# An encoder in four runs: transposing the next run's inputs inside the output projection

## The chip, the core and the metric

The kernel runs on one core of one Trainium2 chip. Times are device microseconds (us) of one execution; lower is better. TensorE (PE) multiplies matrices and writes PSUM, VectorE (DVE) and ScalarE (ACT) read PSUM and work on SBUF, GpSimd (POOL) works on SBUF, and SyncE (SP) issues most transfers. Each engine takes its instructions in program order, and semaphores tie the engines together.

## The reference, cut to what matters

Two batches go through the same two-layer encoder, a prompt of 512 tokens and a sample of 1024 tokens, 1024 features wide.

```
def encoder_layer(x, ...):
    h = x @ w_in                            # 1024 x 2912, cut into twelve parts
    oa = window_attn(...) * silu(a_g)
    ob = mla(...) * silu(b_g)
    oc = neighborhood_attn(...) * silu(c_g)
    o = concatenate([oa, ob, oc]) @ w_out   # 1024 x 1024
    return layer_norm(ALPHA * x + o, ln_g, ln_b)
```

So the kernel has four runs: layer 0 on the prompt (run 0, 512 tokens) and on the sample (run 1, 1024 tokens), then layer 1 on the prompt (run 2) and on the sample (run 3). Run s+1 never reads what run s writes: the input of run s+1 is the output of run s-1 (the input norm for run 1), which lies in HBM in `y_out`.

## The kernel before

**Tiles.** Tokens go in tiles of 128: a run has NT = 4 or 8 of them. Each large product is made of three float32r matmuls: both factors are split into a high part and a low part (`x_hi`, `x_lo`, `w_hi`, `w_lo`), and high x high, high x low and low x high are added up in PSUM. `products` (L562 to L567) issues them all. `x_hi` and `x_lo` hold 1024 token columns and are used twice in a run: first for the run's transposed input, and at its end for the gated attention output.

**Input of a run.** SP loads tile t of the input from HBM into `x_place[t]` (`load_x`, L1362; seven tiles right after the last attention scores of the run before, L1481 to L1483; an eighth shares the place of tile 0 and is loaded at the start of its run, L1409 to L1411). PE transposes a tile with eight 128x128 transposes into two PSUM banks out of banks 4 to 7 (`transposes`, L569 to L576, key "xT"). ACT copies each half into `x_hi` (`high_part`, L791), DVE subtracts that from PSUM into `x_lo` and frees the bank (`low_part`, L1010). In the kernel before all this stands at the start of a run: tiles 0 to 3, then, ahead of the first two pieces of the first weight unit, tiles 4, 5 and 6, 7 (`rest_of_x`, L709 to L713). Ahead of piece 0 PE also waits until tiles 2 and 3 are read (`wait_parts`).

**Weights.** They come in units of 256 columns, twelve for the input projection ("ck" is the first, "aq0" the second) and four for the output projection ("o0" to "o3"). For each unit SP loads two halves, ACT makes `w_hi` (`split_high`, L828) and `w_lo` is made by POOL for half 0 and by DVE for half 1 (`split_low`, L452, the subtraction stands in L456). One exception: at the start of runs 1 to 3 POOL makes both halves of ck (L1282 to L1284). PE waits for both halves before it begins a unit. ck has two pieces of 24 matmuls (128x512) for 512 tokens and four for 1024.

**Output projection and norm.** `out_order` (L160) gives the order of PE's tiles: (0, t) for all t, (1, t) for all t, and then (2, t) and (3, t-1) in turns; each is 24 matmuls (128x256) into one of banks 0 to 3. DVE adds each into `z` (L1217). After (3, t) DVE takes the statistics of token tile t (`norm_stats`), then `norm_coef` of tile t-1 and `norm_gain` of tile t-2, a product with ln_g (L980); ACT makes the square root (`norm_sqrt`, L775) and the scaling (`norm_rows`, L771); POOL adds ln_b (`bias_rows`, `norm_bias`, L1249), and SP stores the tile. The last three tiles' gain and bias stand in the next run (`norm_tail`, L1078; `norm_last_rows`, L820; L1285).

**POOL's order at a boundary**, which this change leaves alone, is:

```
                for i in range(len(IN_UNITS) + 1, NU):
                    split_low(pool, s, i, 0)              # o1, o2, o3, half 0
                pool.wait_ge(lnp_loaded, 32 * (s + 1))
                bias_rows(s, range(NT - 1 if s == RUNS - 1 else NT - 3))
                # next run, i = 0:
                    split_low(pool, s, i, 0)              # ck, half 0
                    if s and i == 0:
                        split_low(pool, s, 0, 1)          # ck, half 1
                        bias_rows(s - 1, range(NTILES[s - 1] - 3, NTILES[s - 1]))
```

So POOL adds the bias of tile 0 (runs of four tiles) or of tiles 0 to 4 (runs of eight) ahead of ck's `w_lo`, the bias of the last three tiles behind it, and then makes aq0's half 0.

Of the kernel before, what the change touches and what calls it, by code (L numbers as in the profile page):

```python
# [29 lines left out]
RUNS = len(SEQ_LEN)  # L30
# [134 lines left out]


def pe_steps(ph, s):


    n = len(units_of(ph, s)) // 2  # L170
    steps = []
    late = 1 if dense_wide(ph, s) else 2
    for j in range(n + late):
        if j < n:
            steps.append(("S", 2 * j))
            if ph != "B":
                steps.append(("S", 2 * j + 1))
        if 0 <= j - 1 < n:
            steps.append(("T", j - 1, 0))
        if j - late >= 2 and (j - late) % 2 == 0:  # L180
            steps.append(("R", (j - late) // 2 - 1))
        if j < n and ph == "B":
            steps.append(("S", 2 * j + 1))
        if 0 <= j - 1 < n and late == 1:
            steps.append(("T", j - 1, 1))
        if 0 <= j - late < n:
            steps.append(("V", j - late))
    return steps + [("R", n // 2 - 1)]
# [17 lines left out]
def encoder_kernel(nc, ins, y_out):  # L206
# [18 lines left out]
    with ctx:  # L225
# [84 lines left out]
        for s, NT in enumerate(NTILES):  # L310
            for t in range(NT):
                for hf in range(2):
                    uses.take(("xT", s, t, hf), 4 + (2 * t + hf) % 4)
            for u in IN_UNITS:
                if u in TOKEN_UNITS:
                    for t in range(NT):
                        take_mm((u, s, t))
                else:
                    for c, j in feature_order(s, u):
                        take_mm((u, s, j, c))  # L320
# [28 lines left out]
            for u, t in out_order(s):  # L349
                take_mm(("out", s, u, t))  # L350

        def halves(s, ph):
# [59 lines left out]
        group_no = Numbered(all_groups)  # L412
        xh_no = Numbered([("xT", s, t, i) for s in range(RUNS) for t in range(NTILES[s]) for i in range(2)])
        split_no = Numbered([(s, u) for s in range(RUNS) for u in UNITS])
# [145 lines left out]
        def _(pe):  # L560
# [138 lines left out]
            for s, NT in enumerate(NTILES):  # L699

                def x_tiles(tiles):
                    for t in tiles:
                        if s:
                            pe.wait_ge(xin_loaded[t], loads_of(t, 1, s))
                        else:
                            pe.wait_ge(pre_ln[4], t + 1)
                        transposes(s, "xT", t)

                def rest_of_x(n):  # L709
                    if n % 2 == 0:  # L710
                        wait_parts(s, "xT", 2 * n)
                    if NT > 4 and n < 2:
                        x_tiles((4 + 2 * n, 5 + 2 * n))  # L713
                if s == 0:
                    pe.wait_ge(ident_loaded, 16)
                x_tiles(range(4))
                if s == 0:
                    pe.wait_ge(pre_const, 16 * 5)
                    nc.tensor.matmul(bank[0][0:A_HEADS, :], t5_sb, onehot, start=True, stop=True).then_inc(pre_mm, 1)
                    pe.wait_ge(pre_neg, 1)  # L720
# [29 lines left out]
                for n, t in out_order(s):  # L750
# [7 lines left out]
                    for h in range(2):  # L758
                        if n == 0 and h == 1:
# [3 lines left out]
                                                             (x_hi[:, k, q_tile(t)], w_lo[:, i % 2, k, :]),  # L763
                                                             (x_lo[:, k, q_tile(t)], w_hi[:, i % 2, k, :]))])


        @block.scalar
        def _(act):
# [4 lines left out]
            def norm_sqrt(sems, k):  # L773
                act.wait_ge(sems[0], k + 1)
                nc.scalar.activation(ln_sd[:, k % 12:k % 12 + 1], ln_mv[:, k % 12, 1:2], ACT.Sqrt, bias=eps[:, 0:1]).then_inc(sems[1], 1)  # L775

            def norm_steps(sems, bufs, k):

                for n, buf in enumerate(bufs):
                    norm_sqrt(sems, k + n)  # L780
                    if n:
                        norm_rows(sems, bufs[n - 1], k + n - 1)

# [58 lines left out]
            for s, NT in enumerate(NTILES):  # L842
                split_high(s, 0)
                for t in range(NT):
                    high_part(s, t)
                if s:
                    norm_last_rows(s - 1)
                split_high(s, 1)
# [100 lines left out]
                split_high(s, NU - 2)  # L949
                split_high(s, NU - 1)  # L950
                norm_steps(layer_ln, [z_place(t) for t in range(NT - 1)], ln_no[s, 0] - 1)
                if s == RUNS - 1:
# [4 lines left out]
        def _(dve):  # L957
# [127 lines left out]
            for s, NT in enumerate(NTILES):  # L1085
                if s == 0:
                    split_low(dve, s, 0, 1)
                for t in range(NT):
                    low_part(s, t)
                if s:  # L1090
                    norm_tail(s - 1)
                split_low(dve, s, 1, 1)
                if s == 0:
# [113 lines left out]
                for n, t in out_order(s):  # L1207
# [11 lines left out]
                    if n == 3:  # L1219
# [6 lines left out]
                        if 1 < t < NT - 1:  # L1226
                            norm_gain(ln_norm, ln_gain, z_place(t - 2), k - 2, qkC[:, 0, :])
                if s == RUNS - 1:
                    norm_tail(s)
# [98 lines left out]
        def _(sp):  # L1328
# [55 lines left out]
            for s, NT in enumerate(NTILES):  # L1384
# [96 lines left out]
                if s + 1 < RUNS:  # L1481
                    for t in range(min(NTILES[s + 1], 7)):
                        load_x(s + 1, t)  # L1483
# [89 lines left out]
```

## Time and profile before

| | us |
|---|---|
| median of 3 runs | 1938.62 |
| lowest, highest | 1937.54, 1939.48 |
| the profiled execution, its time | 1935.7 |
| its span, first to last instruction | 1933.9 |

The time of the profiled execution is its span and 1.8 us around it. Times within the trace count from the span's start. "Boundary 0-1" is the stretch from the last output matmul of run 0 to the steady matmuls of run 1's input projection; boundaries 1-2 and 2-3 likewise.

### The profile page before, as it was taken

To read this page: it belongs to the slowest core of one execution; us is meant where nothing else is said; L and a number is where in the kernel's file an instruction comes from. 1 tells how busy PE (TensorE), PEld (TensorE's weight loads), DVE (VectorE), ACT (ScalarE), POOL (GpSimd) and SP (SyncE) were. 2 spreads that over 40 slices of the span, in tenths; PEclk is the share of its full clock that TensorE was granted. 3 is DMA by queue.
4 is the path that set the end of the run, shared out by engine and by line. 5 is a ranking of instruction groups with operands and counts; after the bars stand their busy time and mean duration, and the time that the engine had idled before them with its cause. 6 is when DMAs were issued, how large, how long until landed. Compare 5 with 4: busy or idle time off the path is not lost.

```text
span 1933.9 us, 31986 instructions
## 1 busy us (share of the span) xinstructions
PE 1830.6 (95%) x12530; PEld 1482.0 (77%) x12530; DVE 957.2 (49%) x2247; ACT 787.9 (41%) x1675; POOL 433.6 (22%) x491
## 2 busy tenths in 40 slices
PE   3999988999999998999989999999999999989996
PEld 2896578889986664889979865888898766578896
DVE  4365654311425875555452475460133287555636
ACT  3344653321124666443142366342112266644512
POOL 3352402310110062001152213140111103500103
PEclk9999999999999999999999999999999999989998
DMA  6666134221126020006145350621212151000222
GB/s 205 208 214 193 26 120 120 76 66 44 45 66 156 9 62 0 1 2 197 45 147 192 103 149 1 202 82 55 66 45 66 49 138 38 25 1 2 84 70 87
DMA packets 148163, 167.15 MB, mean 86 GB/s; under 512 B 18304, under 2 KB 134400, under 8 KB 147504
## 3 DMA queue, kind: packets, MB, share of 16 engines
q1 hardware_dynamic: 146080, 158.75, 27.4%
q0 software_dynamic: 1152, 4.19, 0.5%
q8 instruction: 102, 1.67, 0.4%
q10 hardware_dynamic: 784, 2.16, 0.3%
q14 instruction: 45, 0.37, 0.1%
HBM read 143.00 MB, written 32.65 MB: 91 GB/s over the span
## 4 chain that ended last, share of the span: by engine, by line
PE 87%; DVE 7%; ACT 3%; issue 1%; POOL 1%; DMA 1%; SPq 0%; DVEq 0%; ACTq 0%
PE psum L565 64%; PE psum L685 8%; PE psum L655 8%; PE psum L637 5%; DVE nmax L1025 2%; PE psum L696 1%; DVE pt_sb L1050 1%; ACT pAC L809 1%; DVE x_lo L1016 1%; DVE qB_lo L1182 1%; POOL gT L1249 0%; DMA qA<-x_prompt 0%; PE psum L575 0%; ACT qB_hi L931 0%; PE psum L551 0%
## 5 line engine op out<-in xcount | busy, mean ns | idle before, releaser
L565 PE MATMUL psum<-w_hi,x_hi 128*128 128x256 f32 x1344 | 379.9, 283 | 8.8 <-DVE x_lo L1205 6.7
L565 PE MATMUL psum<-w_hi,x_lo 128*128 128x256 f32 x1344 | 381.0, 284 | 0.0
L565 PE MATMUL psum<-w_lo,x_hi 128*128 128x256 f32 x1344 | 380.6, 283 | 0.0
L565 PE MATMUL psum<-x_hi,w_hi 128*128 128x512 f32 x816 | 325.8, 399 | 10.4 <-DVE hT L1095 7.8
L565 PE MATMUL psum<-x_lo,w_hi 128*128 128x512 f32 x816 | 325.2, 399 | 0.0
L565 PE MATMUL psum<-x_hi,w_lo 128*128 128x512 f32 x816 | 325.2, 398 | 0.0
L456 POOL TENSOR_TENSOR w_lo<-w_stage,w_hi 128x1024 fp32r<-128x1024 f32 (+1 forms) x83 | 164.3, 1990 | 651.1 <-ACT w_hi L839 651.0
L456 DVE TENSOR_TENSOR w_lo<-w_stage,w_hi 128x1024 fp32r<-128x1024 f32 (+1 forms) x77 | 141.4, 1852 | 323.4 <-ACT w_hi L839 323.4
L565 PEld LDWEIGHTS psum<-w_hi,x_hi 128*128 128x128 f32 x1344 | 255.7, 190 | 10.4 <-issue 10.2
L565 PEld LDWEIGHTS psum<-w_lo,x_hi 128*128 128x128 f32 x1344 | 254.4, 189 | 0.2
L565 PEld LDWEIGHTS psum<-w_hi,x_lo 128*128 128x128 f32 x1344 | 253.7, 189 | 0.0
L839 ACT ACTIVATE w_hi<-w_stage 128x1024 fp32r<-128x1024 f32 (+1 forms) x160 | 129.4, 859 | 228.7 <-PE psum L565 160.4
L565 PEld LDWEIGHTS psum<-x_hi,w_hi 128*128 128x128 f32 x816 | 154.8, 190 | 50.2 <-DVE hT L1095 9.5
L816 ACT ACTIVATE pt_sb<-psum 128x256 f32<-128x256 f32 (+2 forms) x224 | 113.4, 506 | 189.2 <-PE psum L655 186.5
L565 PEld LDWEIGHTS psum<-x_hi,w_lo 128*128 128x128 f32 x816 | 154.7, 190 | 37.8
L565 PEld LDWEIGHTS psum<-x_lo,w_hi 128*128 128x128 f32 x816 | 154.8, 190 | 37.3
L1273 POOL COPY rinv_wide<-rinv 128x256 f32<-128x256 f32 x96 | 38.5, 401 | 629.5 <-DVE rinv L1056 629.5
L809 ACT ACTIVATE pAC<-pAC,nmax 128x385 f32<-128x385 f32 (+3 forms) x288 | 164.3, 573 | 22.7 <-DVE nmax L1042 13.3
L1025 DVE TENSOR_REDUCE nmax<-psum 128x1 f32<-128x1024 f32 (+1 forms) x96 | 100.5, 1047 | 122.0 <-PE psum L565 120.6
L655 PEld LDWEIGHTS psum<-ident,pAC 128*128 128x128 f32 x768 | 81.8, 142 | 83.2 <-ACT pAC L809 73.2
L1050 DVE COPY pt_sb<-psum 128x256 f32<-128x256 f32 (+2 forms) x224 | 127.3, 568 | 11.0 <-PE psum L655 11.0
L655 PE MATMUL psum<-ident,pAC 128*128 128x128 f32 x768 | 123.3, 288 | 7.9 <-ACT pAC L809 6.8
(141 smaller groups left out, 2651.7 us busy)
## 6 DMA issues: line engine op xcount, KB each, us to landing
w_stage<-w_in SPq DMA_DIRECT2D x48, 512.0 KB, 4.6
w_stage<-w_in SPq DMA_DIRECT2D x88, 256.0 KB, 3.4
toep<-rpb_tile SPq DMA_DIRECT2D x12, 1152.0 KB, 15.0
rpb_tile<-rpb_col SPq DMA_DIRECT2D x48, 192.0 KB
hT<-y SPq DMA_DIRECT2D x18, 512.0 KB, 12.0
y<-hT SPq DMA_DIRECT2D x18, 512.0 KB, 2.7
w_stage<-w_out SPq DMA_DIRECT2D x32, 256.0 KB, 4.1
w_stage<-w_out SPq DMA_DIRECT2D x16, 512.0 KB, 5.0
```

What stands on the lines that cost most here:

```text
L456: last = eng.tensor_tensor(lo, src, hi.bitcast(F32), ALU.subtract)
L565: last = nc.tensor.matmul(out, w, x, start=(n == 0 and part != 1), stop=(n == len(pairs) - 1 and part != 0))
L637: nc.tensor.matmul(ps[:, 0:n], w, x, start=True, stop=True).then_inc(full(("S", s, u, 0)), 1)
L655: last = nc.tensor.transpose(ps[:, (c % 4) * P:(c % 4 + 1) * P], src[:, c * P:(c + 1) * P], ident[:, :])
L685: last = nc.tensor.matmul(bank[b][64 * k:64 * k + 64, cols], value_tile(s, u, c), pt_sb[:, slot, (c % 4) * P:(c % 4 + 1) * P], start=(c == ...
L696: last = nc.tensor.transpose(bank[b][:, 256 + P * m:256 + P * m + P], rinv_wide[:, P * m:P * m + P], ident[:, :])
L809: nc.scalar.activation(pAC[:, i % 3, 0:m], pAC[:, i % 3, 0:m], ACT.Exp, bias=nmax[:, j:j + 1], scale=-1.0, accum_out=psums[:, j:j + 1]).th ...
L816: nc.scalar.activation(pt_sb[:, half_index[s, (u, hf)] % 4, 0:n], ps[:, 0:n], ACT.Copy).then_inc(pt_act, 1)
L839: last = nc.scalar.activation(hi, src, ACT.Copy)
L1025: nc.vector.tensor_reduce(nmax[:, j:j + 1], b_scores(s, i), AX.XY, ALU.min).then_inc(score_done, 1)
L1050: nc.vector.tensor_copy(pt_sb[:, half_index[s, (u, hf)] % 4, 0:n], ps[:, 0:n]).then_inc(pt_dve, 1)
L1273: nc.gpsimd.tensor_copy(rinv_wide[:, :].rearrange("p (u n) -> p u n", u=4), rinv[:, at:at + 4].unsqueeze(2).broadcast_to([P, 4, 64])).then ...
```

## The change

The next run's tiles are transposed and split while the output projection of the run ahead is under way. `next_x` says which tile follows which output tile: tile t after (3, t) for t up to 3, and, where the next run has eight tiles, tile 4 after (1, 1), tile 5 after (1, 3) and tile 6 after (2, 1). Tile 7 stays at the start of its run, ahead of piece 1 of ck. PE, ACT and DVE each take their part at that place in their own order. ACT's steps of the norm are no longer a block behind `split_high` of o3 but stand in the loop over `out_order`; `split_high` of the next run's ck follows (2, NT-1); `norm_last_rows` and `norm_tail` come first in the next run. SP loads the tiles of a run of 1024 tokens in the order 4, 5, 6, 0, 1, 2, 3. POOL's list of instructions stays as it is.

```
+def x_order(s):
+
+    return (4, 5, 6, 0, 1, 2, 3, 7) if s and NTILES[s] > 4 else tuple(range(NTILES[s]))
+
+
+def next_x(s, n, t):
+
+    if s + 1 == RUNS:
+        return ()
+    if n == 3 and t < min(NTILES[s], NTILES[s + 1]):
+        return (t,)
+    if NTILES[s + 1] > NTILES[s]:
+        return {(1, 1): (4,), (1, 3): (5,), (2, 1): (6,)}.get((n, t), ())
+    return ()
+
+
+def x_at_start(s):
+
+    return (7,) if s and NTILES[s] > 4 else () if s else range(NTILES[s])
...
                     if n % 2 == 0:
                         wait_parts(s, "xT", 2 * n)
-                    if NT > 4 and n < 2:
-                        x_tiles((4 + 2 * n, 5 + 2 * n))
+                    if s and n == 1:
+                        x_tiles(s, x_at_start(s))
                 if s == 0:
                     pe.wait_ge(ident_loaded, 16)
-                x_tiles(range(4))
-                if s == 0:
+                    x_tiles(s, x_at_start(s))
...
                              [p for k in range(4 * h, 4 * h + 4) for p in ((x_hi[:, k, q_tile(t)], w_hi[:, i % 2, k, :]),
...
+                    x_tiles(s + 1, next_x(s, n, t))
...
-                split_high(s, 0)
-                for t in range(NT):
+                if s == 0:
+                    split_high(s, 0)
+                else:
+                    norm_last_rows(s - 1)
+                for t in x_at_start(s):
                     high_part(s, t)
-                if s:
-                    norm_last_rows(s - 1)
                 split_high(s, 1)
...
-                split_high(s, NU - 1)
-                norm_steps(layer_ln, [z_place(t) for t in range(NT - 1)], ln_no[s, 0] - 1)
+                for n, t in out_order(s):
+                    if (n, t) == (1, NT - 1):
+                        split_high(s, NU - 1)
+                    if n == 3 and t < NT - 1:
+                        k = ln_no[s, t] - 1
+                        norm_sqrt(layer_ln, k)
+                        if t:
+                            norm_rows(layer_ln, z_place(t - 1), k - 1)
+                    for x in next_x(s, n, t):
+                        high_part(s + 1, x)
+                    if (n, t) == (2, NT - 1) and s + 1 < RUNS:
+                        split_high(s + 1, 0)
...
-                for t in range(NT):
-                    low_part(s, t)
                 if s:
                     norm_tail(s - 1)
+                for t in x_at_start(s):
+                    low_part(s, t)
                 split_low(dve, s, 1, 1)
...
                             norm_gain(ln_norm, ln_gain, z_place(t - 2), k - 2, qkC[:, 0, :])
+                    for x in next_x(s, n, t):
+                        low_part(s + 1, x)
...
                 if s + 1 < RUNS:
-                    for t in range(min(NTILES[s + 1], 7)):
+                    for t in x_order(s + 1)[:7]:
                         load_x(s + 1, t)
```

The bookkeeping of banks (`take_x`) and of the count of `x_hi` halves (`xh_no`) follows the new order.

## Rows read from the trace of the kernel before

**Rows 1.** Page: the span, and part 1, busy time, share of span and count.

```profile
span 1933.9 us, 31986 instructions
...
PE 1830.6 (95%) x12530; PEld 1482.0 (77%) x12530; DVE 957.2 (49%) x2247; ACT 787.9 (41%) x1675; POOL 433.6 (22%) x491
```

**Rows 2.** Chain that ended last, by time: start, length, engine, tile, line.

```profile
346.98 254.68 PE psum L565 x1368
...
997.15 119.16 PE psum L565 x648
```

**Rows 3.** Timeline, PE, boundary 0-1: start, length, engine, line, names, count [idle before <-releaser].

```profile
329.09 1.91 PE L575 MATMUL psum<-ident,qA 128*128 128x128 f32 x16
333.27 2.36 PE L575 MATMUL psum<-ident,qA 128*128 128x128 f32 x16 [2.27 <-DVE x_lo L1016]
...
339.36 0.48 PE L565 MATMUL psum<-x_hi,w_hi 128*128 128x512 f32 x1
...
345.07 1.04 PE L575 MATMUL psum<-ident,kA 128*128 128x128 f32 x8
345.94 1.04 PE L575 MATMUL psum<-ident,qA 128*128 128x128 f32 x8
346.73 0.48 PE L565 MATMUL psum<-x_hi,w_hi 128*128 128x512 f32 x1
```

**Rows 4.** Timeline, POOL, boundary 0-1.

```profile
330.02 2.36 POOL L1249 TENSOR_TENSOR hT<-hT,qkC 128x1024 f32<-128x1024 f32 x1 [19.47 <-DVE hT L980]
332.35 4.69 POOL L456 TENSOR_TENSOR w_lo<-w_stage,w_hi 128x1024 fp32r<-128x1024 f32 x2
```

**Rows 5.** Windows: length, busy us (count) of each engine, PEclk, DMA share, GB/s.

```profile
294.40:329.10 34.70, 34.70 (x289) 34.61 (x290) 14.46 (x29) 7.93 (x10) 4.79 (x2) 1.00 0.28 81
984.50:987.90 3.40, 3.40 (x10) 2.66 (x9) 3.40 (x3) 1.41 (x4) 3.16 (x1) 0.51 0.49 144
```

**Rows 6.** Timeline, DVE, boundary 0-1: tile (3, 2), its gain, and tile (3, 3).

```profile
326.42 0.42 DVE L1217 SCALAR_TENSOR_TENSOR hT<-hT,psum 128x256 f32<-128x256 f32 x1 [2.46 <-PE psum L565]
...
328.67 1.22 DVE L980 TENSOR_TENSOR hT<-hT,qkC 128x1024 f32<-128x1024 f32 x1
329.80 0.42 DVE L1217 SCALAR_TENSOR_TENSOR hT<-hT,psum 128x256 f32<-128x256 f32 x1
```

**Rows 7.** Timeline, ACT, boundary 0-1: the high parts of tiles 0 to 3.

```profile
331.83 4.44 ACT L794 ACTIVATE x_hi<-psum 128x512 fp32r<-128x512 f32 x8
```

**Rows 8.** Timeline, POOL, boundary 2-3.

```profile
1274.75 4.67 POOL L456 TENSOR_TENSOR w_lo<-w_stage,w_hi 128x1024 fp32r<-128x1024 f32 x2
```

**Rows 9.** Timeline, PE, boundary 2-3: the first matmul of ck's piece 1.

```profile
1289.13 0.48 PE L565 MATMUL psum<-x_hi,w_hi 128*128 128x512 f32 x1
```

**Rows 10.** Timeline, POOL, boundary 1-2.

```profile
975.86 2.37 POOL L1249 TENSOR_TENSOR hT<-hT,qkC 128x1024 f32<-128x1024 f32 x1 [3.38 <-DVE hT L980]
978.18 4.70 POOL L456 TENSOR_TENSOR w_lo<-w_stage,w_hi 128x1024 fp32r<-128x1024 f32 x2
984.74 9.43 POOL L1249 TENSOR_TENSOR gT<-gT,qkC 128x1024 f32<-128x1024 f32 x3 [1.86 <-DVE gT L980]
994.12 2.98 POOL L456 TENSOR_TENSOR w_lo<-w_stage,w_hi 128x512 fp32r<-128x512 f32 x2
```

**Rows 11.** Timeline, DVE, boundary 1-2: one gain alone, and the last three.

```profile
974.57 1.22 DVE L980 TENSOR_TENSOR hT<-hT,qkC 128x1024 f32<-128x1024 f32 x1
...
983.44 5.66 DVE L980 TENSOR_TENSOR gT<-gT,qkC 128x1024 f32<-128x1024 f32 x3
```

**Rows 12.** Timeline, PE, boundary 1-2: matmuls of ck at either clock.

```profile
983.46 0.47 PE L565 MATMUL psum<-x_hi,w_hi 128*128 128x512 f32 x1 [1.93 <-DVE x_lo L1016]
...
985.23 0.63 PE L565 MATMUL psum<-x_hi,w_hi 128*128 128x512 f32 x1
985.66 0.63 PE L565 MATMUL psum<-x_lo,w_hi 128*128 128x512 f32 x1
```

**Rows 13.** Transfers: issue, count, KB each, median us from issue to landing.

```profile
qA<-y SPq DMA_DIRECT2D x14, 512.0 KB, 4.4
```

More of the change, by code:

```diff
@@ L310, in encoder_kernel, with take_x @@
         for s, NT in enumerate(NTILES):
-            for t in range(NT):
+            def take_x(s, t):
                 for hf in range(2):
                     uses.take(("xT", s, t, hf), 4 + (2 * t + hf) % 4)
+            if s == 0:
+                for t in range(NT):
+                    take_x(s, t)
             for u in IN_UNITS:
@@ L318, in encoder_kernel @@
                 else:
-                    for c, j in feature_order(s, u):
+                    for n, (c, j) in enumerate(feature_order(s, u)):
+                        if u == "ck" and n == 1:
+                            for t in x_at_start(s) if s else ():
+                                take_x(s, t)
                         take_mm((u, s, j, c))
@@ L350, in encoder_kernel @@
                 take_mm(("out", s, u, t))
+                for x in next_x(s, u, t):
+                    take_x(s + 1, x)
         def halves(s, ph):
@@ L412, in encoder_kernel @@
         group_no = Numbered(all_groups)
-        xh_no = Numbered([("xT", s, t, i) for s in range(RUNS) for t in range(NTILES[s]) for i in range(2)])
+        xh_no = Numbered([("xT", s, t, i) for s in range(RUNS) for t in x_order(s) for i in range(2)])
         split_no = Numbered([(s, u) for s in range(RUNS) for u in UNITS])
@@ L699, in _, with x_tiles @@
             for s, NT in enumerate(NTILES):
-                def x_tiles(tiles):
+                def x_tiles(s, tiles):
                     for t in tiles:
@@ L775, in norm_sqrt @@
                 nc.scalar.activation(ln_sd[:, k % 12:k % 12 + 1], ln_mv[:, k % 12, 1:2], ACT.Sqrt, bias=eps[:, 0:1]).then_inc(sems[1], 1)
[L777 to L782, printed above, removed]
             act.wait_ge(pre_mem, 2)
@@ L842, in _ @@
             for s, NT in enumerate(NTILES):
-                split_high(s, 0)
-                for t in range(NT):
+                if s == 0:
+                    split_high(s, 0)
+                else:
+                    norm_last_rows(s - 1)
+                for t in x_at_start(s):
                     high_part(s, t)
-                if s:
-                    norm_last_rows(s - 1)
                 split_high(s, 1)
@@ L1087, in _ @@
                     split_low(dve, s, 0, 1)
-                for t in range(NT):
-                    low_part(s, t)
                 if s:
                     norm_tail(s - 1)
+                for t in x_at_start(s):
+                    low_part(s, t)
                 split_low(dve, s, 1, 1)
```

## The prediction

> **What bounds the kernel now.** The page comes first: of a span of 1933.9 us PE is busy for 95% [rows 1], so what PE does not do itself matters only where PE waits. The change touches three such places, the boundaries between runs. In the chain of waits the long PE stretches behind boundaries 0-1 and 1-2 run without a break, 254.68 us from 346.98 and 119.16 us from 997.15 [rows 2]; what arrives late at a boundary is not made up there. So I measure each boundary by one moment: the first matmul of ck's piece 1 at 0-1 (346.73, [rows 3]) and at 2-3 (1289.13, [rows 9]), and the first matmul of aq0 at 1-2 (997.15, [rows 2]). The timelines of PE, POOL and DVE are then read for what sets that moment.
>
> At 0-1 the output matmuls end at 329.09. Transposes follow in blocks with a wait of 2.27 us for `x_lo` in between, ck starts at 339.36, and a second block of 16 transposes, 345.07 to 346.73, parts pieces 0 and 1 [rows 3]. Beside it POOL adds the bias of tile 0 from 330.02 to 332.38, as soon as DVE's gain has run, and makes both halves of ck's `w_lo` by 337.04 [rows 4]. The weights are thus ready 2.3 us ahead of the inputs. That is all the room there is.
>
> **The change, part by part.** *Transposes.* Eight take 345.94 - 345.07 = 0.87 us [rows 3]. None is removed: 64 stay for a run of eight tiles, 32 for one of four. They move into a stretch in which PE is already busy for 34.70 of 34.70 us with a matmul every 0.12 us [rows 5], so each tile put in stretches it by 0.87 us. Bounds: 0, if they slipped into gaps, and 0.87; I take 0.87, since the row shows no gap. What they save is the wait for `x_lo`.
>
> *What stands behind the stretch.* Ahead of (3, 2) at 0-1 lie the transposes of tiles 4, 5, 6, 0 and 1: 5 x 0.87 = 4.35 us. DVE's gain of tile 0 belongs to the step of (3, 2), 2.25 us behind its first instruction [rows 6], and POOL's bias of tile 0 waits for that gain [rows 4]. POOL's order is unchanged and ck's `w_lo` is queued behind that bias. So the weights come 4.35 us later: 337.04 + 4.35 = 341.4. This takes the place of the wait that was removed. ACT's `w_hi` of ck, now behind (2, 3), is earlier than before and of no help, because POOL is held by the bias.
>
> *Boundary 0-1.* PE starts ck at 341.5 (0.1 us for the hand-over), piece 0 takes 345.07 - 339.36 = 5.71 us [rows 3], tile 7's eight transposes 0.87: piece 1 starts at 348.1 against 346.73, **+1.3 us** with rounding. Tile 7's load is issued behind the store of tile 0, at some 337, and lands 4.4 us later [rows 13], well ahead of 347. The next latest is `x_lo` of tile 3: (3, 2) reaches DVE at 326.42 + 4.35 = 330.8; its step takes 329.80 - 326.42 = 3.38 us [rows 6]; `low_part` of tile 2 waits about 0.7 us for ACT (a scaling, then a high part of 4.44/8 = 0.56 us, [rows 7]) and takes as an estimate 1.2; then the step of (3, 3) without a gain, 3.38 - 1.22 = 2.2, and again 1.2: 339.5. So even with weights in time PE would start ck no earlier than it does now.
>
> *Do DVE and ACT keep up?* A step of PE is two output tiles and a transposed one: 48 x 0.12 + 0.87 = 6.6 us. DVE's is 3.38 + 0.42 + 0.7 + 1.2 = 5.7 [rows 6]. They do; with four banks for the output tiles I cost these edits, the new order of `norm_sqrt` and `norm_rows` and the new order of loads at 0. If that cover were gone, PE would stop for a bank.
>
> *Boundary 2-3.* The same shape: `w_lo` ended at 1279.42 [rows 8] and ends at 1283.8; piece 1 starts at 1283.9 + 5.71 + 0.87 = 1290.5 against 1289.13 [rows 9]: **+1.3 us**.
>
> *Boundary 1-2.* Run 2 has four tiles, put behind (3, 0) to (3, 3), so (3, 6), whose step holds the gain of tile 4, comes 4 x 0.87 = 3.5 us later. POOL's bias of tile 4 ended at 978.2 [rows 10] and ends at 981.7. Then `w_lo` of ck, 4.70 us [rows 10]: 986.4 at best. Before, ck started at 983.46 [rows 12]. DVE's last three gains now come right then, no longer behind the `low_part`s. One gain alone takes 1.22 us, three beside POOL's bias took 5.66 [rows 11], while POOL's three biases took 9.43 where three alone take 3 x 2.37 = 7.1 [rows 10]: the two engines hold each other up. Bounds for ck's weights: 986.4 with no gain in between, 986.4 + 2 x 1.22 = 988.8 with two; I take one, 987.6. The Trainium skill (SBUF — State Buffer, section "SBUF: two separate sides") calls the port that DVE and GpSimd share an exclusive lock, which the engine that starts first holds for its whole instruction; the trace agrees, with 5.66 and 9.43 us. Without such a lock this boundary would come out 1.2 us lower.
>
> Two pieces of ck take 2 x 24 x 0.238 (5.71/24) = 11.4 us. Behind an idle PE the clock comes in: between 984.50 and 987.90 the granted clock was 0.51 of full, the 1.2 GHz level, after PE had waited for `x_lo` until 983.46 [rows 5, 12], and a matmul took 985.66 - 985.23 = 0.43 us instead of 0.238. That stretch cost 3.4 x (0.43 - 0.238)/0.43 = 1.5 us. The new wait, from 978.5 to 987.6, is longer than that one, so the 1.5 us stay: ck ends at 987.6 + 11.4 + 1.5 = 1000.5. POOL needs until about the same time: from 978.2 to 997.1 it was idle for 1.86 us [rows 10], so the same work from 981.7 on ends at 998.8, or 1000 with the gain moved in. aq0 starts at 1000.4 against 997.15: **+3.2 us** (bounds +1.6 and +5).
>
> *The clock at 0-1 and 2-3.* Before, waits of 2.27 us between blocks of transposes left it at full [rows 3]. Now PE has nothing from the transposes of tile 3 (about 335.2) to 341.5, over 6 us. Bounds: 0, if the slow stretch falls into the wait itself, and 3.0, two stretches; I take 1.2, near to the 1.5 of the one seen: **+2.4 us** for both. The Trainium skill (TensorE: Matmul & The Clock Gate, "What's actually happening") says that the throttled state is the default and that activity releases it; the stretch at 0.51 behind a wait agrees.
>
> **The sum.** 1.3 + 1.3 + 3.2 + 2.4 = +8.2 us. The profiled execution, 1935.7 us, would take 1943.9. It lies 2.9 us under the median of 1938.62; against the median the forecast is 1946.8 us. A measurement of this kernel can tell a change of 0.2%, 3.9 us, from none.
>
> **The rivals.** *A, the clock stays up and POOL and DVE do not meet.* Then only the waits for POOL are left: 1.3 + 1.3 + 1.6 = +4.2, 1942.8 us. For it: at 0-1 waits of 2.27 us did nothing to the clock. Against it: the new waits are nearly three times as long.
> *B, the transposes slip into PE's queue* and stretch nothing. Then the weights come as before: ck starts at 337.2 and piece 1 at 343.8, -3.0; at 2-3 1279.5 + 6.6 = 1286.1, -3.0; at 1-2 POOL, rid of its 1.86 us of idle time, has aq0's half at about 996, -1.1: -7.1, **1931.5 us, faster**. It decides from the point where a tile stretches the output projection by less than some 0.4 us: 2.3 us of room over five tiles. For it: busy PE need not be PE at its peak. Against it: a matmul every 0.12 us without a gap [rows 5].
> *C, DVE falls behind.* If ACT's scaling delays a high part by over 1 us more, the 0.9 us of room in a step is gone; each of the twelve steps of (3, t) with a transposed tile, four at each boundary, could cost 0.4 us: +5 on top, 1951.8 us. Against it: the sum of 5.7 in 6.6 us.
>
> **Chances.** The forecast 0.66, A 0.16, B 0.08, C 0.10. A lies just past the bound of 0.2%, so most of it counts as no change: faster 0.07, same 0.14, slower 0.79. The range starts below A, less what runs differ by (1 us to either side), and takes in the two upper bounds, +5 at 1-2 and part of C: 1940.0 to 1952.5 us.
>
> **What would show it.** In the changed profile: PE's output stretch longer by 5.2 us (six tiles) at 0-1; POOL's bias of tile 0 at about 334.4 and ck's `w_lo` ending at about 341.4; ck's first matmul released by POOL's `w_lo` and no longer by `x_lo`, at all three boundaries, after an idle stretch of PE of over 6 us; a granted clock of about half behind it. I am wrong if PE's first ck matmul follows the last transposes at once, if the output stretch does not grow, or if the wait is for `x_lo`.

## The result, and the profile after

| | before | changed kernel |
|---|---|---|
| median, us | 1937.54 | 1942.93 |
| lowest, highest | 1933.22, 1941.13 (7 runs) | 1939.94, 1945.58 (7 runs) |
| profiled execution: time, span | 1935.7, 1933.9 | 1941.06, 1939.3 |

The ratio of the two is **1.003 [1.0015, 1.0044]**: slower by 5.4 us, between 2.9 and 8.5. The forecast was +8.2 us, slower.

From the page of the changed kernel, the span and the line of busy times:

```profile
span 1939.3 us, 31986 instructions
...
PE 1828.4 (94%) x12530; PEld 1483.5 (76%) x12530; DVE 957.5 (49%) x2247; ACT 787.7 (41%) x1675; POOL 434.8 (22%) x491
```

As many instructions as before, PE busy for 2 us less, a span longer by 5.4 us [rows 1]: nothing was added, PE waits more. The diff moves line numbers: the products are L595 here (L565 before), the transposes L605 (L575), the low halves of weights L486 (L456), POOL's bias L1285 (L1249), DVE's gain L1014 (L980), `low_part` L1050 (L1016).

The chain of waits at boundary 0-1, then at 1-2 (start, us, what):

```profile
332.78 1.14 DVE hT L1014
...
334.05 2.36 POOL hT L1285
336.42 4.63 POOL w_lo L486 x2
...
341.13 8.25 PE psum L595 x24
...
350.26 254.68 PE psum L595 x1368
...
987.28 3.37 issue
990.65 132.34 PE psum L595 x696
```

In the chain of before [rows 2] the long stretch began at 346.98; here it begins at 350.26 and is just as long. What leads to it reads as a sentence: DVE's gain of tile 0, POOL's bias of tile 0, POOL's two low halves of ck, PE. At 0-1 the transposes of the other tiles no longer stand in the chain.

PE's timeline at the three boundaries (start, length, what; in brackets the idle time ahead of it and what ended it):

```profile
341.13 0.77 PE L595 MATMUL psum<-x_hi,w_hi 128*128 128x512 f32 x1 [6.10 <-POOL w_lo L486]
341.70 0.63 PE L595 MATMUL psum<-x_lo,w_hi 128*128 128x512 f32 x1
...
346.39 0.43 PE L595 MATMUL psum<-x_hi,w_hi 128*128 128x512 f32 x1
...
350.01 0.48 PE L595 MATMUL psum<-x_hi,w_hi 128*128 128x512 f32 x1
...
990.65 0.76 PE L595 MATMUL psum<-x_hi,w_hi 128*128 128x512 f32 x1 [8.74 <-issue]
...
1291.11 0.76 PE L595 MATMUL psum<-x_hi,w_hi 128*128 128x512 f32 x1 [6.09 <-POOL w_lo L486]
```

ck waits for 6 to 9 us at each boundary. Before there were two waits of about 2 us each, for `x_lo`, with a block of transposes in between [rows 3, 12]. Behind the wait the matmuls run 0.63 us long, and start 0.43 apart, until 346.39, then 0.39 to 0.40 long.

The windows over those slow stretches, and over the output stretch of run 0 (busy time and count of PE, PEld, DVE, ACT, POOL, then granted clock, DMA share, GB/s):

```profile
339.50:346.30 6.80, 5.17 (x12) 4.13 (x13) 6.80 (x4) 1.24 (x1) 5.64 (x3) 0.51 0.67 199
984.60:994.80 10.20, 4.14 (x10) 3.31 (x11) 10.08 (x6) 3.73 (x5) 10.20 (x5) 0.51 0.51 159
1288.40:1295.20 6.80, 4.09 (x10) 3.25 (x11) 6.76 (x7) 2.20 (x2) 5.63 (x3) 0.51 0.83 241
294.18:333.88 39.70, 39.70 (x336) 39.70 (x336) 20.76 (x39) 15.54 (x22) 4.81 (x2) 1.00 0.27 73
```

The granted clock is at the 1.2 GHz level behind all three waits; in the first profile of before only behind the one at 1-2 [rows 5]. The output stretch, 34.70 us in before [rows 5], is 39.70 long and still full.

POOL's timeline at 0-1 and 1-2:

```profile
334.05 2.36 POOL L1285 TENSOR_TENSOR hT<-hT,qkC 128x1024 f32<-128x1024 f32 x1 [23.63 <-DVE hT L1014]
336.37 4.66 POOL L486 TENSOR_TENSOR w_lo<-w_stage,w_hi 128x1024 fp32r<-128x1024 f32 x2
...
982.62 2.34 POOL L1285 TENSOR_TENSOR hT<-hT,qkC 128x1024 f32<-128x1024 f32 x1 [3.35 <-DVE hT L1014]
984.92 5.64 POOL L486 TENSOR_TENSOR w_lo<-w_stage,w_hi 128x1024 fp32r<-128x1024 f32 x2
990.52 9.51 POOL L1285 TENSOR_TENSOR gT<-gT,qkC 128x1024 f32<-128x1024 f32 x3
```

and DVE's, the last low parts at 0-1 and the last three gains at 1-2:

```profile
338.02 1.28 DVE L1050 TENSOR_TENSOR x_lo<-psum,x_hi 128x512 fp32r<-128x512 f32 x2
...
985.19 9.76 DVE L1014 TENSOR_TENSOR gT<-gT,qkC 128x1024 f32<-128x1024 f32 x3
```

At 1-2 DVE's gains and POOL's low halves run beside each other: the two low halves take 5.64 us in place of 4.66, and the three gains, which also meet POOL's biases, 9.76 in place of 3 x 1.22.

**All profiles in one table.** I cut each trace at the same matmuls of PE, counted from the start of the kernel, and took the time from cut to cut. "0-1" runs from the first matmul of output tile (1, 0) to the first of ck's third piece, "1-2" from the first of (3, 0) to the first of the unit behind aq0, "2-3" like 0-1. "3a" is run 3 from there to the matmul at 1669.66 in before, "3b" from that to the one at 1840.00. Worked out from PE's timelines; us:

```
                       0-1     1-2     2-3      3a      3b
before               58.11   73.82   58.36   374.82  170.34
before, again        60.24   74.31   60.42   374.82  170.33
changed              61.54   77.20   61.07   373.35  166.80
changed, again       61.08   76.59   61.08   373.35  166.85
e1                   60.49   76.74   60.66   373.34  171.01
e2                   59.22   76.49   59.22   373.35  170.00
e3                   60.29   78.12   61.35   373.34  168.71
e3, again            62.07   77.99   59.21   373.36  170.82
e4                   57.47   73.41   57.47   373.34  168.77
f1                   52.84   75.56   52.83   373.34  170.97
f2                   52.83   73.54   52.75   373.34  170.11
```

Between the two first profiles the boundaries cost 3.43 + 3.38 + 2.71 = +9.5 us, and run 3 gives 1.47 + 3.54 = 5.0 of it back; the +0.9 that is missing to the 5.4 of the spans lies elsewhere, most of it in run 2. Between the two second profiles the boundaries cost only 0.84 + 2.28 + 0.66 = +3.8, run 3 gives 5.0 back, and the changed kernel is the shorter one by 0.5 us. One pair of profiles is thus no measure of the whole; the ratio above, of seven executions each, is. Run 3 has no run behind it, and the change does nothing in these two stretches: the granted clock decides it (below).

### The profile page after: what moved, and what is told of

Same layout as the page of the kernel before. It is cut to its first block, busy times and chain, and to the rows that moved or that the text cites. A ratio compares the mean times of both kernels' runs of the same rounds, so it can differ in the third digit from the quotient of the medians.

```text
span 1939.3 us, 31986 instructions
## 1 busy us (share of the span) xinstructions
PE 1828.4 (94%) x12530; PEld 1483.5 (76%) x12530; DVE 957.5 (49%) x2247; ACT 787.7 (41%) x1675; POOL 434.8 (22%) x491
## 4 chain that ended last, share of the span: by engine, by line
PE 88%; DVE 6%; ACT 3%; issue 1%; POOL 1%; DMA 1%; SPq 0%; DVEq 0%; ACTq 0%; POOLq 0%
PE psum L595 64%; PE psum L715 8%; PE psum L685 8%; PE psum L667 5%; DVE nmax L1059 2%; PE psum L726 1%; DVE pt_sb L1084 1%; ACT pAC L832 1%; PE psum L605 1%; POOL w_lo L486 1%; DVE qB_lo L1216 0%; DMA qA<-x_prompt 0%; PE psum L581 0%; ACT qB_hi L955 0%; POOL hT L1285 0%
## 5 line engine op out<-in xcount | busy, mean ns | idle before, releaser
L595 PE MATMUL psum<-w_hi,x_hi 128*128 128x256 f32 x1344 | 381.4, 284 | 8.2 <-DVE x_lo L1239 6.7
L595 PE MATMUL psum<-w_hi,x_lo 128*128 128x256 f32 x1344 | 381.0, 283 | 0.0
L595 PE MATMUL psum<-w_lo,x_hi 128*128 128x256 f32 x1344 | 380.2, 283 | 0.0
L595 PE MATMUL psum<-x_hi,w_hi 128*128 128x512 f32 x816 | 328.0, 402 | 29.1 <-POOL w_lo L486 12.2
L595 PE MATMUL psum<-x_lo,w_hi 128*128 128x512 f32 x816 | 326.8, 401 | 0.0
L595 PE MATMUL psum<-x_hi,w_lo 128*128 128x512 f32 x816 | 326.7, 400 | 0.0
L486 POOL TENSOR_TENSOR w_lo<-w_stage,w_hi 128x1024 fp32r<-128x1024 f32 (+1 forms) x83 | 166.2, 2012 | 673.7 <-ACT w_hi L862 673.6
L486 DVE TENSOR_TENSOR w_lo<-w_stage,w_hi 128x1024 fp32r<-128x1024 f32 (+1 forms) x77 | 134.4, 1762 | 335.0 <-ACT w_hi L862 334.9
L595 PEld LDWEIGHTS psum<-w_hi,x_hi 128*128 128x128 f32 x1344 | 255.5, 190 | 9.6 <-issue 9.4
L595 PEld LDWEIGHTS psum<-w_lo,x_hi 128*128 128x128 f32 x1344 | 254.7, 189 | 0.2
L595 PEld LDWEIGHTS psum<-w_hi,x_lo 128*128 128x128 f32 x1344 | 253.6, 189 | 0.0
L595 PEld LDWEIGHTS psum<-x_hi,w_hi 128*128 128x128 f32 x816 | 156.1, 191 | 69.2 <-issue 21.5
L595 PEld LDWEIGHTS psum<-x_hi,w_lo 128*128 128x128 f32 x816 | 155.8, 191 | 38.3
L595 PEld LDWEIGHTS psum<-x_lo,w_hi 128*128 128x128 f32 x816 | 156.2, 191 | 37.7
```

Of the source, the lines that this page charges most:

```text
L486: last = eng.tensor_tensor(lo, src, hi.bitcast(F32), ALU.subtract)
L595: last = nc.tensor.matmul(out, w, x, start=(n == 0 and part != 1), stop=(n == len(pairs) - 1 and part != 0))
```

## Experiments

Two theories. **Mine:** the loss is PE's wait for POOL, which is held by the bias of the first tile, and the clock that falls behind the wait. **Rivals:** the transposes cost more inside the output projection than outside it, or the new order of ACT, DVE or SP costs by itself.

### e1: POOL makes ck's low halves ahead of the bias

```
                 for i in range(len(IN_UNITS)):
-                    split_low(pool, s, i, 0)
+                    if s == 0 or i:
+                        split_low(pool, s, i, 0)
...
-                        split_low(pool, s, 0, 1)
...
-                bias_rows(s, range(NT - 1 if s == RUNS - 1 else NT - 3))
+                if s == RUNS - 1:
+                    bias_rows(s, range(NT - 1))
+                else:
+                    ahead = 3 if NT > 4 else 0
+                    bias_rows(s, range(ahead))
+                    split_low(pool, s + 1, 0, 0)
+                    split_low(pool, s + 1, 0, 1)
+                    bias_rows(s, range(ahead, NT - 3))
```

> The changed kernel, with POOL's two low halves of ck moved ahead of the bias it was queued behind (ahead of tile 0's bias in runs of four tiles; between the biases of tiles 2 and 3 in run 1); the last three biases and aq0's half stay behind it. Theory (ck's weights are late because POOL makes them behind a bias that the inserted transposes delay): at 0-1 ck starts at about 339.6 instead of 341.13, now released by DVE's x_lo of tile 3, and piece 1 at 346.2 to 348.6 (the clock), instead of 350.01; at 2-3 the same gain; at 1-2 ck starts at about 983 instead of 990.65 and aq0 at about 999 instead of 1003.93. About 4 to 6 us under the changed kernel, so -2 to +2.5 us against the kernel before. Rival (the stretch itself or the new order of DVE and ACT costs the time, and POOL's order is no matter): +4 to +6 us against the kernel before, as in the changed kernel.

Measured: 1943.48 us, ratio 1.0026 [1.0015, 1.0038] to before. The forecast, -2 to +2.5 us against the kernel before, failed: at 0-1 and 2-3 ck no longer waits for POOL, and yet next to nothing was won. PE's timeline and POOL's:

```profile
339.95 0.77 PE L595 MATMUL psum<-x_hi,w_hi 128*128 128x512 f32 x1 [5.16 <-DVE x_lo L1050]
...
981.37 0.47 PE L595 MATMUL psum<-x_hi,w_hi 128*128 128x512 f32 x1 [0.87 <-issue]
...
1000.44 0.80 PE L595 MATMUL psum<-x_hi,w_hi 128*128 128x512 f32 x1 [7.59 <-POOL w_lo L486]
```

```profile
981.23 5.75 POOL L1285 TENSOR_TENSOR hT<-hT,qkC 128x1024 f32<-128x1024 f32 x2
988.13 8.92 POOL L1285 TENSOR_TENSOR gT<-gT,qkC 128x1024 f32<-128x1024 f32 x3 [1.16 <-DVE gT L1014]
997.01 3.38 POOL L486 TENSOR_TENSOR w_lo<-w_stage,w_hi 128x512 fp32r<-128x512 f32 x2
```

At 0-1 the next to be late is `x_lo` of the last tiles: the wait shrinks from 6.10 to 5.16 us. At 1-2 ck starts within 0.87 us of the output projection, but POOL's biases are now ahead of aq0's half, and aq0 waits 7.59 us. So POOL's order makes ck's wait, but `x_lo` ends only 1 us earlier, and at 1-2 the wait for POOL moves on to aq0. The clock falls behind each of these waits; in the table the boundaries are 1.0, 0.5 and 0.4 us shorter than in the changed kernel.

### e2: PE is kept busy in the wait

```
+                if s:
+                    ps = wait_free(pe, ("ck", s, 0, 0))
+                    for _ in range(70 if s == 2 else 48):
+                        nc.tensor.transpose(ps[:, 0:P], ident[:, :], ident[:, :])
```

These transposes of the identity, ahead of ck, write a bank that ck then overwrites.

> The changed kernel with idle PE time filled: while PE waits for ck's weights it makes transposes of the identity into ck's own bank, 48 at 0-1 and 2-3 (48 x 0.109 = 5.2 us of some 6 us of waiting), 70 at 1-2 (7.6 of 8.7 us), and the first real matmul overwrites them. Theory (part of the loss is the granted clock, which falls behind the long wait): piece 0 of ck takes 5.7 us instead of 8.1 at 0-1 and 5.7 instead of 7.6 at 2-3, and ck's 13.3 us at 1-2 become 11.4, of which aq0's weights on POOL (ready at 1003.0) let 0.9 through. Sum 2.4 + 1.9 + 0.9 = 5 us under the changed kernel, so 0 to +2 us against the kernel before; ck's start itself does not move. Rival (the slow matmuls come from something else, or the added work delays ck): no gain or a loss, +5 us or more against the kernel before.

Measured: 1939.98 us, ratio 1.0003 [0.9992, 1.0015], as expected. PE's timeline at 0-1, and the window from ck's start to its second piece:

```profile
336.18 5.40 PE L754 MATMUL psum<-ident 128*128 128x128 f32 x48
342.51 0.47 PE L595 MATMUL psum<-x_hi,w_hi 128*128 128x512 f32 x1 [0.92 <-issue]
```

```profile
342.51:349.00 6.49, 6.49 (x32) 5.34 (x33) 5.46 (x3) 0.15 (x1) 5.42 (x2) 1.00 0.62 202
```

ck starts as late as in the changed kernel, 7.32 us behind the start of the last output matmul (342.51 - 335.19; there 341.13 - 333.88 = 7.25), but at a granted clock of 1.00. From ck's start to its second piece it takes 6.49 us in place of 350.01 - 341.13 = 8.88. This parts the loss: by the table the waits alone cost 1.1 at 0-1, 2.7 at 1-2 and 0.9 at 2-3 against the first profile of before, and the clock the rest, 2.3, 0.7 and 1.9. At 1-2 the parting is blurred, because that profile of before has 3.4 us at the half clock there itself [rows 5] and e2 none. It rests on one profile each: against the second profile of the changed kernel the clock's part is 1.9, 0.1 and 1.9. The profiled execution of e2 as a whole was no shorter than the changed kernel's (1941.84 and 1941.06 us), since 3b, where nothing differs, took 3.2 us more; the ratio, of twelve executions, is the better witness.

### e4: only the columns that are free early stay interleaved

```
-    if n == 3 and t < min(NTILES[s], NTILES[s + 1]):
-        return (t,)
+    if n == 3 and t == NTILES[s] - 1:
+        return tuple(range(min(NTILES[s], NTILES[s + 1])))
```

Tiles 4, 5 and 6 stay where the change puts them; tiles 0 to 3 are transposed behind the last output matmul.

> The changed kernel with part of the move undone: tiles 4, 5 and 6 stay within the output projection, tiles 0 to 3 are transposed behind its last matmul, as before. Theory (each tile ahead of the step that holds the gain delays POOL's weights by 0.87 us, and a long idle PE loses the clock): at 0-1 the weights come 3 x 0.87 = 2.6 us later than before, at 339.7, x_lo of the four tiles at about 340; ck starts at 340.0, piece 1 at 346.6 (346.73 before), and PE's waits are broken up by transposes, so the clock stays up; 2-3 likewise; 1-2 as before. -1.5 to +1.5 us against the kernel before. Rival (the loss comes with the new order of ACT's and DVE's norm steps or of SP's loads, which stay): +4 to +6 us against the kernel before.

Measured: 1935.76 us, ratio 0.9985 [0.9975, 0.9995], a little faster than before. PE at 0-1, and the windows over the boundaries 0-1 and 1-2:

```profile
337.89 0.47 PE L595 MATMUL psum<-x_hi,w_hi 128*128 128x512 f32 x1 [1.93 <-POOL w_lo L486]
```

```profile
329.72:350.00 20.28, 16.47 (x91) 13.40 (x90) 17.50 (x24) 11.47 (x19) 17.83 (x8) 1.00 0.51 176
972.46:1005.60 33.14, 27.10 (x131) 21.55 (x130) 20.77 (x24) 14.06 (x23) 21.92 (x10) 1.00 0.51 152
```

The wait ahead of ck is as short as in before again, and the clock stays at 1.00 over both boundaries. The interleaving of tiles 4 to 6, the new order of norms and loads, and the interleaved transposes as such cost nothing here; the loss belongs to tiles 0 to 3, which stand ahead of the step with the gain and leave a long idle stretch behind it. The rivals fall: that tiles 0 to 3 cost no more inside the projection than outside is read from its length, 5.0 us more for six tiles, 0.83 each, against 0.87 before.

### e3 and its repeat: POOL's order of e1 in the kernel before

The diff is that of e1.

> The kernel before, with POOL's order alone changed in the same way as in e1. Theory (before, POOL's weights came ahead of the inputs, and the wait for them was made by the change): nothing at 0-1 and 2-3, where x_lo still sets ck's start, and 0 to +2 us at 1-2, where POOL has the same work ahead of aq0: within 0.15% of the kernel before. Rival (POOL's order costs time by itself, whatever the transposes do): 2 us or more faster than the kernel before.

Measured: 1944.26 us, ratio 1.0034 [1.0021, 1.0047]. I had expected no change. It was profiled a second time:

> The kernel before with POOL's new order, profiled a second time, to see what of its 6 us belongs to the order. Theory (the order takes 1 to 2 us at 1-2, where the biases run later beside DVE's gains, and the rest is the clock, which falls in other places in this execution): aq0 at 1-2 again waits for POOL's low halves, 1 to 2 us later against ck's first piece than in the kernel before, and the two stretches at the half clock among the transposes of 0-1 and 2-3 are gone or elsewhere. Rival (the order itself costs at 0-1 and 2-3): these boundaries are again 2 to 5 us longer than in the two profiles of the kernel before.

The second execution took 1943.04 us. At 1-2 both are alike, 78.12 and 77.99 us in the table against 73.82 and 74.31: aq0 waits for POOL, which now adds five biases beside DVE's gains ahead of aq0's half (the second row is the kernel before at this place):

```profile
1001.91 0.47 PE L565 MATMUL psum<-x_hi,w_hi 128*128 128x512 f32 x1 [3.16 <-POOL w_lo L456]
```

```profile
997.15 0.50 PE L565 MATMUL psum<-x_hi,w_hi 128*128 128x512 f32 x1 [0.69 <-POOL w_lo L456]
```

So about 4 us belong to the order, at 1-2; that is more than the 1 to 2 I had put down. Some 2.5 us of them are aq0's later start, counted from the first matmul of (3, 0); 1.5 are a stretch of 3.4 us at the half clock that stands behind this wait in both executions, and in neither profile of the kernel before. At 0-1 and 2-3 the two executions differ by about 2 us in opposite ways (60.29 and 62.07, 61.35 and 59.21), and 62.07 and 61.35 lie clearly above both profiles of the kernel before. PE's waits there are, within 0.01 us, those of the second profile of before (2.27 and 1.72, next section). What differs is the time at the half clock: 6.8 and 6.8 us in the first execution of e3, 10.2 and 3.4 in its repeat, 6.8 and 3.4 in that profile of before. So the order adds no wait there; whether it makes the slow stretches longer, two executions can't tell. e1 has the same order, so its price at 1-2 is part of why e1 won so little.

### The two kernels again

> The kernel before, unchanged, profiled a second time. Theory (whether the granted clock falls behind a wait differs from execution to execution, at the same waits): the waits ahead of ck and aq0 stand at the same places with the same lengths within 0.3 us, while the stretches at about half of the granted clock stand elsewhere than in the first profile, where one boundary of three (1-2) had one, and each one more or less moves the boundary's end by 1.5 to 2.5 us; span within 6 us of 1933.9. Rival (the clock falls by the kernel's own pattern): the same stretches at the same places, and e3's slower boundaries are then due to its order of POOL alone.

> The changed kernel, unchanged, profiled a second time. Theory (the waits belong to the change, where the clock falls to the execution): ck waits for POOL's low halves at all three boundaries, 6.1, 8.7 and about 6 us within 0.3 us, while the stretches at the half clock behind them, three of three in the first profile, are one to three here; each one missing makes its boundary 1.2 to 2.5 us shorter. Rival (a wait of this length always brings the clock down): three of three again.

The kernel before took 1943.85 us in this execution. Its windows at 0-1, 1-2 and in run 3, and two blocks of transposes at 0-1, with the second of them as it was in the first profile:

```profile
333.90:340.70 6.80, 5.08 (x25) 4.59 (x25) 4.25 (x8) 3.56 (x6) 3.08 (x2) 0.50 0.87 268
982.50:989.30 6.80, 5.19 (x19) 4.04 (x17) 6.49 (x11) 5.93 (x10) 4.46 (x3) 0.50 0.61 177
...
1712.90:1723.10 10.20, 10.05 (x27) 7.72 (x28) 3.67 (x3) 3.19 (x6) 0.00 (x0) 0.50 0.01 2
```

```profile
333.21 3.15 PE L575 MATMUL psum<-ident,qA 128*128 128x128 f32 x16 [2.26 <-DVE x_lo L1016]
338.07 3.25 PE L575 MATMUL psum<-ident,qkC 128*128 128x128 f32 x16 [1.72 <-DVE x_lo L1016]
```

```profile
337.67 1.94 PE L575 MATMUL psum<-ident,qkC 128*128 128x128 f32 x16 [2.04 <-DVE x_lo L1016]
```

The wait of 2.27 us [rows 3] is there again (2.26), but this time the clock is at half behind it, and 16 transposes take 3.15 and 3.25 us in place of 2.36 and 1.94. 0-1 and 2-3 are 2.1 us longer each. (Another 3 us of this execution are a transfer: a load of output weights that took 12.23 us, in run 2.) So the kernel before loses clock at its boundaries as well, in some executions.

The changed kernel took 1943.38 us. Its waits are 6.10, 8.74 and 6.11 us, and the clock fell behind all three again. Its window over run 3's attention:

```profile
1709.00:1790.00 81.00, 74.84 (x628) 61.28 (x628) 45.75 (x60) 41.25 (x69) 1.60 (x4) 1.00 0.00 1
```

No half clock, as in its first profile; in both of before there is a stretch of 10.2 us at half level here, and in the seven profiles of the other kernels stretches that add up to 6.8 to 13.7 us. The clock is what gives 3.5 us back (3b in the table); the 1.47 of 3a is a stretch of 3.4 us that only the two profiles of before have. Why just this kernel is spared at 3b, twice of twice, I could not settle.

### f1 and f2: a version that fills the wait

The runs say what a good order needs: something for PE to multiply right behind the last output matmul. f1 turns ck's pieces round in runs of eight tiles. Tokens 512 to 1023 come first, and their tiles 4 to 7 have columns that are free early.

```
 def feature_order(s, u):
-    return [(c, j) for c in range(SEQ_LEN[s] // 512) for j in range(1 if u == "ak" else 2)]
+    late_first = s and NTILES[s] > 4 and u == "ck"
+    return [(c, j) for c in ((1, 0) if late_first else range(SEQ_LEN[s] // 512)) for j in range(1 if u == "ak" else 2)]
...
-    return (4, 5, 6, 0, 1, 2, 3, 7) if s and NTILES[s] > 4 else tuple(range(NTILES[s]))
+    return (4, 5, 6, 7, 1, 2, 3, 0) if s and NTILES[s] > 4 else tuple(range(NTILES[s]))
...
+        return {(1, 1): (4,), (1, 3): (5,), (2, 1): (6,), (2, 2): (7,), (3, 3): (1, 2)}.get((n, t), ())
...
-    return (7,) if s and NTILES[s] > 4 else () if s else range(NTILES[s])
+    return (3, 0) if s and NTILES[s] > 4 else () if s else range(NTILES[s])
```

Beside this PE waits for all four tiles of a half ahead of its first piece, POOL makes ck's low halves ahead of biases as in e1 and aq0's half ahead of the last three, and SP loads aq0 ahead of the stores.

> Against the kernel before. Theory (what is lost lies in PE's idle time ahead of ck, filled by POOL's queue and by the last tiles' splitting; the transposes cost the same wherever they stand): tiles 4 to 7 are transposed in the output projection and their half of ck is multiplied first, so ck starts right behind the last output matmul, without a wait of more than 1 us at 0-1 and 2-3; the four other tiles are transposed behind it (tiles 1 and 2) or ahead of ck's second piece (tiles 3 and 0). At 0-1 and at 2-3 the end of ck comes about 5 us earlier than in the kernel before, at 1-2 aq0 about 5 us earlier, with next to no stretch at the half clock: -14 us, near 1924 us. Rival (the time of the boundary is set by DVE's and POOL's tail, whatever order PE takes): the waits come back ahead of ck's second piece or ahead of aq0, 3 to 6 us each, and the clock falls behind them: -3 to +2 us, 1935 to 1940 us.

Measured: 1926.55 us, ratio **0.9935 [0.9919, 0.995]**, some 12.6 us faster than before where 14 were expected. 0-1 and 2-3 are 5.3 and 5.5 us shorter than in the first profile of before, as expected; 1-2 is not. Two rows of PE and two of SP's queue at 1-2:

```profile
988.87 0.77 PE L596 MATMUL psum<-x_hi,w_hi 128*128 128x512 f32 x1 [3.15 <-issue]
1004.97 0.47 PE L596 MATMUL psum<-x_hi,w_hi 128*128 128x512 f32 x1 [3.24 <-issue]
```

```profile
988.25 5.44 SPq L1413 DMA_DIRECT2D y<-gT  x3
...
995.80 2.25 SPq L1392 DMA_DIRECT2D w_stage<-w_in  x4
```

aq0 begins 8.3 us earlier than in before (997.15), 5.3 of them won at 0-1, and then PE stands before the next unit, whose load SP issued only behind the last three stores. f2 moves the load ahead of them:

```
-                    if s and i == 1:
+                    if s and i == 2:
                         store_y(s - 1, range(NTILES[s - 1] - 3, NTILES[s - 1]))
```

> f1 with one edit: SP issues the load of the unit behind aq0 ahead of the last three stores of the run before. Theory (what f1 lost at 1-2 is this load alone: it was issued at 995.8 behind the stores, landed at 999.9, and PE waited until 1004.97, while aq0 had begun 8.3 us earlier than in the kernel before): the load is issued some 9 us earlier, at about 986, the weights are split by about 996, and the matmuls behind aq0 follow without a wait: 3.5 to 5 us less than f1, 1921.5 to 1923 us, ratio to the kernel before 0.9915 to 0.992. Rival (POOL's three biases, held up by DVE's gains, set the moment whatever SP does): the wait stays within 1 us, 1925.5 to 1927 us.

Measured: 1922.1 us, ratio **0.992 [0.9904, 0.9936]**, 15.5 us faster than before by the ratio. PE at 0-1 and 1-2:

```profile
331.12 1.91 PE L606 MATMUL psum<-ident,qA 128*128 128x128 f32 x16
332.79 0.48 PE L596 MATMUL psum<-x_hi,w_hi 128*128 128x512 f32 x1
...
338.49 1.91 PE L606 MATMUL psum<-ident,qA 128*128 128x128 f32 x16
340.15 0.48 PE L596 MATMUL psum<-x_hi,w_hi 128*128 128x512 f32 x1
...
972.08 0.47 PE L596 MATMUL psum<-x_hi,w_hi 128*128 128x512 f32 x1 [0.86 <-issue]
...
986.70 0.77 PE L596 MATMUL psum<-x_hi,w_hi 128*128 128x512 f32 x1 [3.14 <-issue]
```

At 0-1 PE runs through without a wait. At 1-2 3.14 us are left ahead of aq0, with the clock at half behind them; so 1-2 as a whole takes 73.54 us, hardly less than before (73.82), although aq0 starts 3.0 us earlier in it. Against f1 the moved load is worth 2.0 us at 1-2 in the table. The medians of f1 and f2 differ by 4.5 us, the ratios to the kernel before by 2.9; what the load gave beyond the 2.0 isn't shown.

## Why the prediction was right, and where its sizes were off

**The mechanism holds, step by step.** The output stretch grew as forecast: six tiles x 0.87 = 5.2, measured 39.70 - 34.70 = 5.0, and PE never stopped in it, so transposes do not slip into its queue (rival B falls), and DVE did not fall behind (rival C falls). POOL's bias of tile 0 was due at about 334.4 and came at 334.05; `w_lo` was due at 341.4 and ended at 341.03; ck started at 341.13, forecast 341.5. The last `x_lo` at 0-1 ended at 338.02 + 1.28 = 339.3, forecast 339.5. At 1-2 all lies 3.28 us later, by what came before; aq0 started at 1003.93, without that at 1000.65, forecast 1000.4. ck's wait is for POOL's `w_lo` at 0-1 and 2-3 by name; at 1-2 the row names "issue", 0.1 us after `w_lo` ended (984.92 + 5.64 = 990.56).

**The sum, term by term**, first profile against first profile: 0-1 and 2-3 with their clock 1.3 + 1.2 = 2.5 each, measured 3.43 and 2.71; 1-2 3.2, measured 3.38. e2 parts these: the waits came out a little smaller than forecast (1.1 and 0.9 for 1.3), the clock larger (2.3 and 1.9 for 1.2). The clock stayed low over 6.8 us, not 3.4, of which a part lay in the wait. The two errors offset each other in part, which brings the 8.2 of the sum nearer to the 9.5 of this pair than its terms are.

The direction, the mechanism and the range held. **The term that was off** is the clock's: "Before, waits of 2.27 us between blocks of transposes left it at full [rows 3]." This was true of the one execution that I had. The second profile of before has the same waits with the clock at half behind them, 2.1 us dearer at each of the two boundaries. In the second pair of profiles the boundaries differ by 3.8 us and not by 9.5. A base that sometimes pays the same price can make the difference of medians smaller than the difference of two profiles. And the sum had no term for the clock elsewhere: run 3 is 5.0 us shorter in both profiles of the changed kernel, although the change does nothing there. In the two pairs of profiles the boundaries and run 3 together make +4.5 and -1.2 us, and the spans differ by +5.4 and -0.5. That they are also what makes the medians differ by 5.4 and not by 9.5 is likely but not shown: two profiles a kernel can't tell it. The Trainium skill (TensorE: Matmul & The Clock Gate, "What's actually happening") says of the slow matmuls at a kernel's start that their number varies between runs of one kernel and shouldn't be fitted to a count; the pairs of profiles here show the like at boundaries (6.8, 3.4 or no slow us at the same place). That should have widened my bounds for the clock, on the side of the kernel before too.

**Rival A** gave 1942.8, next to the measured 1942.93, but for another reason than its own: the clock did fall, and POOL and DVE did meet. The rows of that meeting are POOL's low halves at 5.64 us in place of 4.66 and DVE's three gains at 9.76 in place of 3.7.

## What to carry to other kernels

Moving work off an idle stretch of PE wins only what the next engine to be late allows; follow the queue of each engine past the moved instructions, and ask what PE has to multiply when they are gone. Here four tiles moved ahead of the step that POOL waits for, and their saving came back as a longer wait; choosing first the half of the work whose inputs are ready early, with POOL's and SP's order fitted to it, and then moving one load ahead of the stores, gave 15.5 us. The parts of f1 were not measured one by one. Before a term is put down to the clock, look at two profiles of the unchanged kernel.

## What the runs showed of the hardware

The granted clock of 0.5 behind a wait of about 2 us comes in one execution and not in the next: the same 16 transposes behind a wait of 2.27 us took 2.36 and 3.15 us. Behind waits of 6 to 9 us it came six times out of six in the changed kernel. Filling the wait with transposes whose result nobody reads kept the clock at 1.00 and was worth 4.9 and 3.8 us at the three boundaries, against the two profiles of the changed kernel (ratios 1.0003 against 1.003).

A long wait of PE is not needed for the half clock. In run 3's attention, in the second profile of before, the clock fell at 1712.9, after four blocks of transposes with waits of 0.9 to 1.5 us between them, and stayed at 0.50 for 10.2 us in which PE was busy for 10.05. In the second profile of the changed kernel the same blocks with the same waits left it at 1.00. What decides between the two no run here shows.

DVE's gains and POOL's biases of 128x1024 hold each other up: beside each other a gain took 9.76 / 3 = 3.25 us and a bias 9.51 / 3 = 3.17, in place of 1.22 and 2.37 alone.
